# Thirty-two tokens leave the dense U product: row fetches and VectorE sums in the routing, twenty rows in the one-hot stretch

## The reference, cut to what matters

```
q = (hf @ wq).reshape(T, 8, 2, 128)
s = einsum('thcd,hcnd->thcn', q, subkeys)
sv, si = top_k(s, 16)                          # each half of the key
cand = sv[:, :, 0, :, None] + sv[:, :, 1, None, :]
fv, fpos = top_k(cand.reshape(T, 8, 256), 16)  # 16 experts per token and head
gates = softmax(fv)
act = gelu(einsum('chkd,cd->chk', U[fidx], xc))
y = einsum('chk,chkd->cd', gates * act, V[fidx])
```

## Time and profile before

| what | value |
|---|---|
| profiled execution | 1799.91 us |
| its span | 1798.2 us |
| median of the runs | 1799.27 us |
| PE busy | 1731.4 us, 96% |
| DVE busy | 1412.4 us, 79% |
| ACT / POOL busy | 695.4 us / 603.5 us |
| chain that ended last | PE 73%, DMA 2%, DVE 1% |
| L1489 in the chain | 26% |
| 16 DMA engines | 444.37 MB, 247 GB/s on average |

### The profile page before, as it was taken

One profiled execution on the slowest core, in us unless ns is written; L12 is line 12 of the kernel. 1 busy time (PEld: TensorE's weight loads), 2 busy tenths in 40 slices (PEclk: granted clock), 3 DMA queues, 4 the chain that ended last, 5 costly groups with the idle time before them and its releaser, 6 DMA issues.

```text
span 1798.2 us, 36538 instructions
## 1 busy us (share of the span) xinstructions
PE 1731.4 (96%) x12400; PEld 1515.6 (84%) x12400; DVE 1412.4 (79%) x2928; ACT 695.4 (39%) x1304; POOL 603.5 (34%) x481
## 2 busy tenths in 40 slices
PE   5999899889999999899999999999999999999996
PEld 3776788747999999899999999999888888888885
DVE  1885666646878888899999999687698888888877
ACT  3433455514444454433333333334343333333331
POOL 5012633303344353444333343353243332233200
PEclk8999999999999999999999999999999999999998
DMA  9841000254443434699999998999999999999981
GB/s 318 278 155 48 2 3 3 79 202 163 129 135 122 129 123 127 238 321 322 322 327 348 321 317 307 326 411 368 367 412 349 358 351 350 357 357 349 349 281 63
DMA packets 247871, 444.37 MB, mean 247 GB/s; under 512 B 85522, under 2 KB 158580, under 8 KB 247780
## 3 DMA queue, kind: packets, MB, share of 16 engines
q1 hardware_dynamic: 207968, 300.07, 48.0%
q0 software_dynamic: 39168, 142.62, 21.2%
q10 hardware_dynamic: 644, 0.52, 0.2%
HBM read 388.16 MB, written 54.53 MB: 246 GB/s over the span
## 4 chain that ended last, share of the span: by engine, by line
PE 73%; DMA 2%; DVE 1%; SPq 1%; ACT 1%; issue 0%; ACTq 0%; POOL 0%; DVEq 0%
PE bank L1489 26%; PE bank L2030 10%; PE bank L2031 10%; PE bank L2032 10%; PE bank L1469 6%; PE bank L1952 5%; PE bank L2009 4%; PE bank L1427 2%; DMA vsel<-in_peer_v,picks 1%; PE bank L1964 1%; SPq L1460 1%; DMA xrows<-xpicks 0%; DMA uraw<-in_peer_u,xrows 0%; DMA urows<-in_peer_u 0%; DVE n_stats L1393 0%
## 5 line engine op out<-in xcount | busy, mean ns | idle before, releaser
L1489 PE MATMUL bank<-hh,uh 128*128 128x368 f32 x1024 | 350.4, 342 | 0.0
L1489 PE MATMUL bank<-hl,uh 128*128 128x368 f32 x1024 | 337.4, 329 | 0.0
L2030 PE MATMUL bank<-vh,wh 128*128 128x512 f32 x768 | 299.8, 390 | 3.1 <-DVE wl L2443 3.1
L2031 PE MATMUL bank<-vl,wh 128*128 128x512 f32 x768 | 299.6, 390 | 0.0
L2032 PE MATMUL bank<-vh,wl 128*128 128x512 f32 x768 | 299.6, 390 | 0.0
L1547 POOL DMA_INDIRECT vsel<-in_peer_v,picks x128 | 154.2, 1204 | 406.8 <-DVE gt L1573 392.5
L2183 ACT ACTIVATE vh<-vraw 128x1024 fp32r<-128x1024 f32 x128 | 135.9, 1062 | 285.7 <-PE bank L2032 269.6
L1547 POOL DMA_INDIRECT wide<-in_peer_u,picks x108 | 152.6, 1413 | 202.3 <-DVE wide L1554 188.1
L2440 DVE TENSOR_TENSOR vl<-vraw,vh 128x1024 fp32r<-128x1024 f32 x128 | 156.5, 1223 | 80.2 <-ACT vh L2183 80.2
L1489 PEld LDWEIGHTS bank<-hl,uh 128*128 128x128 f32 x1024 | 193.1, 189 | 0.0
L1489 PEld LDWEIGHTS bank<-hh,uh 128*128 128x128 f32 x1024 | 192.8, 188 | 0.0
(11 more groups left out here) (379 smaller groups left out, 2989.1 us busy)
## 6 DMA issues: line engine op xcount, KB each, us to landing
urows<-in_peer_u SPq DMA_DIRECT2D x128, 512.0 KB, 8.2
vraw<-in_peer_v SPq DMA_DIRECT2D x128, 512.0 KB, 6.3
scored<-act_out SPq DMA_DIRECT2D x128, 192.0 KB, 5.2
gates<-SS SPq DMA_DIRECT2D x16, 1536.0 KB, 14.7
gtile<-gates SPq DMA_DIRECT2D x32, 768.0 KB, 7.5
act_in<-scored SPq DMA_DIRECT2D x128, 192.0 KB, 6.3
wt<-in_w_in SPq DMA_DIRECT2D x19, 512.0 KB, 4.4
wq<-in_peer_wq SPq DMA_DIRECT2D x18, 512.0 KB, 3.9
```

The source lines that it names most:

```text
L1489: last = pe.matmul(bank, u[:, k, :], h[:, k, 0:TU], start=(n == 0), stop=(n == 3 * KD - 1))
L2030: pe.matmul(b, wh[s][:, cols], vh[s][:, half], start=first, stop=False)
L2031: pe.matmul(b, wh[s][:, cols], vl[s][:, half], start=False, stop=False)
```

## The change

`TU` falls from 368 to 336. Tokens 336 to 367 (`EARLY` = 32) get their U products from gathered rows, while the routing runs. For one head they need 32 tokens x 16 picks = 512 rows, four fetches of 128 (`REPEAT` = `PER_HEAD` = 4: partition 32 b + t holds token t, pick 4 b + k). After each head DVE writes `ypicks` (the expert numbers of that head, 128 x 16), SP copies them with four small DMAs into `rows_of`, POOL fetches four tiles into `vsel[0..3]`, and DVE forms four dots with `hy` **inside the next head's top-k**, between the sum of candidates and the second top-k. Head 7's four fetches and the sixteen of the extra tokens are made in the one-hot stretch: none in turn 0, two each in turns 1 to 8, one each in turns 9 to 12.

POOL's place for the fetches: after the last `remainder` of an iteration and before the first of the next.

```diff
-        scored = nc.dram_tensor("scored", [NKEYS, P, TD], F32, kind="Internal").ap()
+        scored = nc.dram_tensor("scored", [NKEYS, P, TU], F32, kind="Internal").ap()
...
-TU = TD - EXTRA
-XPAIRS = 2
-XTURNS = EXTRA - XPAIRS
+EARLY = 32
+TU = TD - EXTRA - EARLY
+REPEAT = P // EARLY
+PER_HEAD = TOPK // REPEAT
+LATE_ROWS = PER_HEAD + EXTRA
+XTURNS = 12
+XPAIRS = LATE_ROWS - XTURNS
+FETCHED = HEADS * PER_HEAD + EXTRA
...
+            def head_picks(h):
+                sp.wait_ge(picked, START + h + 1)
+                for b in range(REPEAT):
+                    sp.dma_start(rows_of[EARLY * b:EARLY * (b + 1), bass.ds(PER_HEAD * h, PER_HEAD)],
+                                 ypicks[P - EXTRA - EARLY:P - EXTRA, PER_HEAD * b:PER_HEAD * (b + 1)])\
+                        .then_inc(yrows_in, 16)
...
+            routed(0)
+            with sp.Fori(1, ROUTED) as i:
+                routed(i)
+                head_picks(i - 1)
...
+            def head_rows(h):
+                if h == 0:
+                    pool.wait_ge(xrows_in, START + 16 * copies)
+                else:
+                    pool.wait_ge(xdot_up, START + PER_HEAD * h)
+                pool.wait_ge(yrows_in, START + 16 * REPEAT * (h + 1))
+                for k in range(PER_HEAD):
+                    row_fetch(vsel[k], PER_HEAD * h + k, sel.vs_in[k])
+            for i in range(ROUTED - 1):
                 for s in range(4):
                     scores.remainder(pool, i + OPEN, s)
                     if s in (1, 2):
                         query_rest(i + 1, s - 1)
-            with pool.Fori(OPEN + ROUTED - 1, SPREAD) as i:
+                if i:
+                    head_rows(i - 1)
+            for i in range(OPEN + ROUTED - 1, SPREAD):
                 for s in range(4):
                     scores.remainder(pool, i, s)
+                if i == OPEN + ROUTED - 1:
+                    head_rows(HEADS - 2)
...
+            def row_dot(buf, landed, n, h, column):
+                dve.wait_ge(landed, 16 * n + 16)
+                dve.scalar_tensor_tensor(out=buf[:, :], in0=buf[:, :], scalar=1.0, in1=h[:, :], op0=ALU.mult,
+                                         op1=ALU.mult, accum_out=rdots[:, bass.ds(column, 1)]).then_inc(xdot_up, 1)
...
                     settled(dve.tensor_tensor(cand[:, :, :, :], ...
+                    if not (first and k == 0):
+                        for f in range(PER_HEAD):
+                            row_dot(vsel[f], sel.vs_in[f], h - 1, hy, PER_HEAD * h + (f - PER_HEAD))
...
                     emit_pick(dve, step, cand, cand2, sif, IS, JS, h)
-                    dve.sem_inc(picked, 1)
+                    dve.wait_ge(yrows_in, START + 16 * REPEAT * h)
+                    dve.scalar_tensor_tensor(out=ypicks[:, :], ...).then_inc(picked, 1)
...
+            spread_turn(SPREAD, 0, None)
+            paired = SPREAD + 1 + PER_HEAD // 2
+            for i in range(SPREAD + 1, paired):
+                spread_turn(i, 2, hy)
+            with dve.Fori(paired, SPREAD + 1 + XPAIRS) as i:
+                spread_turn(i, 2, hx)
+            with dve.Fori(SPREAD + 1 + XPAIRS, SPREAD + 1 + XTURNS) as i:
+                spread_turn(i, 1, hx)
...
+            dve.memset(act_in[:, :, TU:TD], 1.0).then_inc(xact_up, 1)
```

More of the change, by code:

```diff
@@ L1848, in _, with row_fetch @@
                 query_rest(0, c)
-            with pool.Fori(0, ROUTED - 1) as i:
+            def row_fetch(into, column, landed):
+                pool.indirect_dma_start(out=into[:, :], out_offset=None, in_=sel.rows[0],
+                                        in_offset=bass.IndirectOffsetOnAxis(ap=rows_of[:, column:column + 1], axis=0))\
+                    .then_inc(landed, 16)
+            def head_rows(h):
[7 more added lines that the diff above has]
+            for i in range(ROUTED - 1):
                 for s in range(4):
@@ L2011, in spread_turn @@
                         last.then_inc(spread, 1)
-            with pe.Fori(SPREAD, SPREAD + XTURNS) as i:
+            with pe.Fori(SPREAD, SPREAD + XTURNS + 1) as i:
                 spread_turn(i)
-            for i in range(SPREAD + XTURNS, CLEAR):
-                spread_turn(i, i == SPREAD + XTURNS)
+            for i in range(SPREAD + XTURNS + 1, CLEAR):
+                spread_turn(i, i == SPREAD + XTURNS + 1)
             with pe.Fori(CLEAR, LAST) as i:
@@ L2266, in _, with head_pair @@
             dve.wait_ge(iota_up, START + 1)
-            with dve.Fori(0, HEADS // 2) as g:
-                chain.enter(g, 2 * per)
+            def head_pair(g, first):
+                chain.local, chain.loop = 0, (g, 2 * per)
                 step = stepper(dve, chain)
@@ L2314, in _ @@
                     emit_pick(dve, step, cand, cand2, sif, IS, JS, h)
-                    dve.sem_inc(picked, 1)
+                    dve.wait_ge(yrows_in, START + 16 * REPEAT * h)
+                    dve.scalar_tensor_tensor(out=ypicks[:, :],
+                                             in0=IS[:, NT - 2, bass.ds(h, 1), :].rearrange("p o k -> p (o k)"),
+                                             scalar=float(NKEYS),
+                                             in1=JS[:, NT - 2, bass.ds(h, 1), :].rearrange("p o k -> p (o k)"),
+                                             op0=ALU.mult, op1=ALU.add).then_inc(picked, 1)
                 assert chain.local == 2 * per, chain.local
-                chain.leave(HEADS // 2)
+            head_pair(0, True)
+            with dve.Fori(1, HEADS // 2) as g:
+                head_pair(g, False)
+            chain.leave(HEADS // 2)
             soft = stepper(dve, Tally(p_soft))
```

145 lines of the change are left out of this document (82 added, 63 removed).

## The result

| | before | after |
|---|---|---|
| median, us | 1798.65 (1797.14 to 1799.43) | 1847.04 (1841.93 to 1852.50) |
| ratio, 95% interval | | 1.0274 (1.0258 to 1.0291) |
| profiled execution, its span | 1799.91, 1798.2 | 1846.64, 1844.9 |
| routing: head 7's `JS` ends | 727.2 | 790.6 |
| turn 0's first product | 735.5 | 799.1 |

The change makes the kernel 48 us slower. The stages (profiled executions, us of the span) say where: turn 0 comes 63.6 us later, then the one-hot stretch gives back 12.6 (401.8 between its first and last spread step, now 389.2) and groups 26 to 31 give back 5.1 (118.5, now 113.4). The V stage is unchanged. The forecast was 1857: +60.9 to turn 0, +1.8, -5. (The 63.6 and the 12.6 come from slightly different cuts; in one cut, from turn 0's first product to turn 15's last, the stretch gives back 11.0.)

The account below looks back on a forecast made before the run. PE was taken to bound the kernel nearly throughout. Routing +61.8, handover -0.9, one-hot stretch +1.8, groups 26 to 31 -5.0 sum to +57.7: median 1857 us, range 1805 to 1880 (8 in 10), likeliest case 1835 to 1872 (0.60).

Parts of the forecast that it names:

- Before the routing, and head 0: Up to head 0's end: shorter steps bring head 0's scores 1.2 us sooner, at 466.4; head 0 takes 28.3 us.
- Head 1: VectorE stands 11 us for late rows: Routing, head 1: SP sends head 0's picks late, DVE stands 11 us before the first dots; head ends at 546.
- Heads 2 to 5 of 41.3 us through blocks on the sums: Routing: 32.9 us of DVE work, +1.3 on the sum of candidates, +7.1 on four dots held by POOL's subtractions.
- Heads 6 and 7 of 38.9: Routing's last two heads: no query weights to subtract, so 38.9 us each; head 7 ends at 789.0, +61.8.
- GpSimd's tie to the picks puts its block beside the sums: Routing: subtractions wait behind fetches, these behind picks, so four subtractions meet the dots: 11.7 us instead of 4.6.
- DVE need not wait for rows from head 2 on: Routing, heads 2 to 7: rows land from 9 us into the next head, wanted at 11.8, so no wait.
- rival 3: Rows late as well: first row lands 15.6 us after a head's end, up to 24 us more, 1881; chance 0.12.
- Handover -0.9: From head 7's end to turn 0: ACT's exponential begins 1.3 us after DVE instead of 2.2, -0.9 us.
- PE's idle and clock: Profile after: PE idle about 10 us per head in the routing and again before turn 0; granted clock below 1.
- One-hot stretch +1.8: Turn 0 unchanged, turns 1 to 8 at 26.0 us (+7.6), turns 9 to 12 -2.8, turns 13 to 15 -1.0 each.
- rival 1: DVE-bound without blocking: dots slip between POOL's subtractions, heads of 32.9 us, total 1809; chance 0.15.
- Rival 2: Faster: DVE's slack carries the heads, only head 1's stall stays, later stages give back 14.5 and 8.4; 1786, chance 0.13.

Follow-up runs that it names:

- ready: Changed kernel with GpSimd fetching, for every head, the rows that head 0 picked, so it never waits for a head's picks: 1852.09 us.
- thin_pool: Changed kernel with GpSimd's subtractions of the routing cut to one eighth of their columns, fetches and waits as they are: 1821.54 us.
- one_input: Changed kernel with the routing's 28 row sums made from the fetched row alone, by an operation with one SBUF input, same place and waits: 1825.06 us.
- narrow: Kernel before with its product narrowed to 336 columns and nothing else, the 32 tokens' scores left out of the result: 1774.07 us.
- shared: Changed kernel with the routing's row sums taken from VectorE: GpSimd makes the products, ScalarE sums them; 1849.17 us.
- tail: Changed kernel with each head's four sums behind the next head's picks (head 6's ahead of head 7's pick products), VectorE's head-pair loop written out: 1820.87 us.
- sixteen_tail: Changed kernel with 16 early tokens instead of 32, two sums a head behind the picks, VectorE's loop written out: 1792.83 us, ratio 0.9969 to the kernel before.
- unrolled: Changed kernel with VectorE's loop over the head pairs written out, nothing else: 1838.61 us.

## Why the prediction was right

The time lies in its range and in the likeliest case's own (1835 to 1872), 10 us below the point. The core of the mechanism is shown: sums with two SBUF inputs and GpSimd's subtractions hold each other, and VectorE becomes the bound of the routing. That head 7 ends at 790.6 against 789.0 is in part luck: blocks in heads 2 to 7 are 36.4 us, not the 45.6 forecast, and a loop's turn that the prediction did not have (5.9) and head 1 (2.9) fill most of the gap.

- **Before the routing, and head 0.** Right: scores at 467.0 against 466.4, head 0 ends at 494.7 as worked out. A product of 24 steps takes 3.69 us, so 32 columns are worth 0.31 us, not 0.35: between 336 and 368 columns the cost is 0.40 ns a column, less than what the earlier trace rows gave between 368 and 512.
- **Head 1: VectorE stands 11 us for late rows.** Right in kind, 13.6 by measurement; the head ends at 548.9 against 546. By its own terms the four dots end at 520.5 + 4.6 + 2.4 = 527.5, not 528.5, a slip of 1 us.
- **Heads 2 to 5 of 41.3 us through blocks on the sums.** The sum is right (40.7, 40.9, 42.2, 38.7) and shown by taking away either side of the pair: one SBUF input, or a short subtraction, brings the heads to 36. Its parts were off. The sums lose 5.7 us on average, not 7.1; the 1.3 us that I gave to the candidates' sum fall on the cast ahead of it (1.1 to 1.4 in heads 2, 3 and 5, none in head 4); and 2.9 us of head 4 are the loop's turn, which the prediction did not have.
- **Heads 6 and 7 of 38.9.** 40.6 and 38.6. Head 6 again holds a turn of the loop, 3.0 us.
- **GpSimd's tie to the picks puts its block beside the sums.** Half of this failed. The tie is there (103.8 us of waits), but `ready` takes it away and the heads stay at 40.7. That VectorE has left the phase (its place in time against GpSimd) in which the subtractions met only operations that are not held fits all runs, but was not tried by itself.
- **DVE need not wait for rows from head 2 on.** Only because blocks made it late. In `thin_pool`, where the sums come when they were worked out to come, rows are 2 to 3 us late in heads 2, 3 and 5. That is rival 3 in small, hidden in the changed kernel.
- **Handover -0.9.** From head 7's `JS` to turn 0 it takes 8.5 us as against 8.3: +0.2.
- **PE's idle and clock.** PE is idle 54.8 us between 495 and 790, 2.5 to 17.4 at a time, so nearer 8 than 10 a head, and 10.5 before the handover's first transposes, where it waits for VectorE. The granted clock is 0.91 in 495 to 790 (before: 1.00), as foreseen in kind, and 0.50, the 1.2 GHz level, from 790 to 803, in and behind that idle. Turn 0's first 12 matmuls take 3.36 us for it, and 1.85 once the clock is back.
- **One-hot stretch +1.8.** The term that was mis-sized: -12.6 by the spread steps in this execution. Turn 0 does not keep its time. In the kernel before it waited on the way for the first extra row (760.15 - 735.53 = 24.6 us to its last product); without that row it takes 819.19 - 799.13 = 20.1, so -4.6. Turns 1 to 8 take 25.25 us each and not 26.0, so -6.0 against the sum: one turn of before, 26.43 us, was taken for all eight, which run from 24.3 to 26.7. Turns 9 to 15 take 23.72, in place of 24.15 and 23.85: -2.1. In this cut, from turn 0's start to turn 15's last product, the stretch gives back 11.0. Only turn 0's part comes again each time. The eight other runs with 32 early tokens have the same code here. In their profiled executions turn 0 takes 18.7 to 21.1 us, but turns 1 to 8 take 25.3 to 26.1 each, 25.8 or more in six of the eight, near the 26.0 of the forecast; the whole cut takes 388 to 398 us, against 399 before. So the stretch gives back 1 to 11 us from one execution to another, for a reason that is not shown.
- **Groups 26 to 31 -5.** Right: 118.7 us in the same cut against "about 118".
- **Rivals.** No run went rival 1's way (heads of 32.9 without blocks): even 28 sums that nothing holds (`one_input`) leave heads of 36.4. Rival 2 would have needed 13 of the 25 us that `narrow` gains without a single new fetch or sum.

What stays open: what sets the length of the one-hot stretch in one execution or another; why an operation slips in between two back-to-back subtractions at one time (the sums of head 3, one for one) and at another is held by four or six in a row (11.11 and 13.31 us in `shared`); and what brings the blocks of `tail` from 12 us to 2 between heads 3 and 4. None was tried apart.

## What to carry to other kernels

Where two engines hold each other up, an engine's idle time can be worth more than its length: with it gone, the places where the two meet change. (No run shows that idle time alone keeps them in phase; `sixteen_tail` keeps its phase while VectorE never waits for scores.) Before giving an engine more work, list which of its instructions can be held (here: those with two SBUF inputs, casts, copies and plain `tensor_scalar`) and where the other engine's operations fall once the idle time is gone. New work belongs where the other engine waits anyway, and in small pieces: half the tokens, the sums behind the picks and the loop written out, together, turned a loss of 48 us into a gain of 6.

## What the runs showed of the hardware

- A VectorE cast of 128x128 elements takes 0.22 us alone, 1.34 to 2.06 in five of the eight heads of the changed kernel, where it meets GpSimd's subtractions of 128x1024, and 13.31 at worst, in `shared`, behind a row of six subtractions and products of GpSimd.
- A `tensor_scalar` with accumulator output over 128x1024 takes 1.22 us inside a subtraction of GpSimd, a `scalar_tensor_tensor` with two SBUF inputs up to 3.4. MAX and index instructions that begin inside a subtraction are at most 0.02 us longer.
- GpSimd pays too: its subtractions beside the sums take 3.24 to 3.40 us instead of 2.35 to 2.42.
- The turn of VectorE's long loop over head pairs costs 2.9 to 3.0 us where nothing covers it; with the loop written out it is gone (`unrolled`).
- TensorE's first 12 matmuls of 336 columns in turn 0, at a granted clock of 0.50 after 10.5 us of idle, take 3.36 us; at 1.00 they take 1.85.
